# Weight slots 128 bytes instead of 64 bytes behind a multiple of 1024, in a one-core fp32 kernel of two model blocks

## What is computed

```python
# first block
h = rms_norm(x); proj = h @ w_in                       # 2048 x 6448
y = concat([rwkv7_mixer(proj_a), gdn_mixer(proj_b)])
x = x + y @ w_out                                      # 2048 x 2048
h = rms_norm(x)
x = x + (silu(h @ ffn_w_gate) * (h @ ffn_w_up)) @ ffn_w_down
x = rms_norm(x)
# second block
x = x + fox_mixer(rms_norm_2(x))                       # w_in 2048 x 6160, w_out 2048 x 2048
x = x + conv_ffn(rms_norm_2(x))                        # w_up 2048 x 11264, w_down 5632 x 2048
```

## Time and profile before

| | |
|---|---|
| median of three runs | 2491.35 us (2488.3 to 2492.03) |
| the profiled execution, its own time | 2490.99 us |
| its span, first to last instruction | 2489.3 us |
| mean granted TensorE clock | 0.995 of full |
| TensorE busy (matmul) | 2437.2 us |
| TensorE busy (weight loads, beside it) | 2409.3 us |
| VectorE, ScalarE, GpSimd busy | 1477.2, 1123.4, 114.8 us |
| moved by DMA | 431.72 MB, mean 173 GB/s |

### The profile page before, as it was taken

The page is one execution under the profiler, slowest core; times in us unless marked ns, Lnnn a source line. Parts: engine busy times, 40 slices in busy tenths (PEclk is TensorE's granted clock), DMA queues, the critical chain, the costliest instruction groups (busy, mean ns, idle before and its releaser), DMA issues.

```text
span 2489.3 us, 57370 instructions
## 1 busy us (share of the span) xinstructions
PE 2437.2 (98%) x24650; PEld 2409.3 (97%) x24650; DVE 1477.2 (59%) x1686; ACT 1123.4 (45%) x1064; POOL 114.8 (5%) x93
## 2 busy tenths in 40 slices
PE   8999989989999999999999999999999999999999
PEld 8999978889999999999999999989999999999998
DVE  5557588664654545554444567674576666765444
ACT  5333524444544444443344544363555555544332
POOL 3000050000200000000020100000200000000000
PEclk9999989999999999999999999999999999999999
DMA  7555300126555555556565565625555555555554
GB/s 233 187 193 195 119 2 4 37 86 188 197 191 192 196 186 197 190 191 196 188 198 191 188 239 200 221 83 188 187 199 189 191 197 186 197 190 190 197 190 150
DMA packets 171387, 431.72 MB, mean 173 GB/s; under 512 B 17614, under 2 KB 23387, under 8 KB 170107
## 3 DMA queue, kind: packets, MB, share of 16 engines
q1 hardware_dynamic: 170027, 422.30, 50.3%
q10 hardware_dynamic: 1232, 7.52, 0.8%
HBM read 427.59 MB, written 2.17 MB: 173 GB/s over the span
## 4 chain that ended last, share of the span: by engine, by line
PE 92%; DVE 6%; ACT 1%; POOL 1%; issue 0%; DMA 0%; DVEq 0%; SPq 0%; ACTq 0%; POOLq 0%
PE ps L1970 29%; PE ps L1971 29%; PE ps L1972 28%; PE ps L2124 1%; POOL SQ L528 1%; DVE TM L1366 0%; DVE LO L1370 0%; DVE TT L1367 0%; DVE CV L1400 0%; ACT HIW L606 0%; DVE LOW L1083 0%; DVE GT L1382 0%; PE ps L2162 0%; DVE TMP L1313 0%; PE ps L2068 0%
## 5 line engine op out<-in xcount | busy, mean ns | idle before, releaser
L1083 DVE TENSOR_TENSOR LOW<-RAW,HIW 128x2048 fp32r<-128x2048 f32 (+1 forms) x396 | 910.3, 2299 | 915.4 <-ACT HIW L606 915.4
L1970 PE MATMUL ps<-H_ROWS,HIW 128*128 128x256 f32 x4928 | 1366.7, 277 | 4.5 <-DVE H_ROWS L1122 1.3
L1971 PE MATMUL ps<-H_ROWS,HIW 128*128 128x256 f32 x4928 | 1365.6, 277 | 0.0
L1972 PE MATMUL ps<-H_ROWS,LOW 128*128 128x256 f32 x4928 | 1364.5, 277 | 0.0
L606 ACT ACTIVATE HIW<-RAW 128x2048 fp32r<-128x2048 f32 (+1 forms) x396 | 759.4, 1918 | 1180.1 <-PE ps L1972 1170.4
L1970 PEld LDWEIGHTS ps<-H_ROWS,HIW 128*128 128x128 f32 x4928 | 927.1, 188 | 6.2 <-issue 4.6
L1972 PEld LDWEIGHTS ps<-H_ROWS,LOW 128*128 128x128 f32 x4928 | 927.8, 188 | 0.0
L1971 PEld LDWEIGHTS ps<-H_ROWS,HIW 128*128 128x128 f32 x4928 | 926.5, 188 | 0.1
L1970 PE MATMUL ps<-HID,HIW 128*128 (+1 forms) x1408 | 388.7, 276 | 0.0
L1971 PE MATMUL ps<-HID,HIW 128*128 (+1 forms) x1408 | 388.6, 276 | 0.0
L1972 PE MATMUL ps<-HID,LOW 128*128 (+1 forms) x1408 | 388.6, 276 | 0.0
(11 more groups left out here) (367 smaller groups left out, 1514.1 us busy)
## 6 DMA issues: line engine op xcount, KB each, us to landing
RAW<-in_ffn_w_up SPq DMA_DIRECT2D x264, 512.0 KB, 4.3
RAW<-in_ffn_w_down SPq DMA_DIRECT2D x176, 512.0 KB, 4.8
RAW<-in_fox_w_in SPq DMA_DIRECT2D x98, 512.0 KB, 4.4
RAW<-in_w_in SPq DMA_DIRECT2D x96, 512.0 KB, 4.1
RAW<-in_ffn_w_gate SPq DMA_DIRECT2D x88, 512.0 KB, 3.6
RAW<-in_w_out SPq DMA_DIRECT2D x32, 512.0 KB, 5.0
RAW<-in_fox_w_out SPq DMA_DIRECT2D x32, 512.0 KB, 4.6
INV<-rows_out ACTq DMA_DIRECT2D x4, 1024.0 KB, 7.3
```

Of the source, the lines that this page charges most:

```text
L1083: V.tensor_tensor(LOW[:, u_const % 4, 0:n], RAW[:, u_const % 4, 0:n], HIW[:, u_const % 2, 0:n].bitcast(F32), ALU.subtract).then_inc(lo_mad ...
L1970: mm(o_, hi_w, h_hi, start=start, stop=False)
L1971: mm(o_, hi_w, h_lo, start=False, stop=False)
L1972: i = mm(o_, lo_w, h_hi, start=False, stop=stop)
```

## The change

Two offsets change from 64 to 128 bytes. The raw and low slots and all tensors with addresses relative to `w0` move up by 64 bytes, and so do the high slots. X, H_ROWS, HID and everything behind the 256 spare bytes stay where they are. The instructions, their order, their waits and the DMAs' sizes are the same.

```diff
-        w0 = o + 64
+        w0 = o + 128
         RAW = at("RAW", [P, RAW_SLOTS, UNIT], w0)
         LOW = at("LOW", [P, RAW_SLOTS, UNIT], w0, F32R); o += 32768
-        HIW = at("HIW", [P, HI_SLOTS, UNIT], o + 64, F32R); o += 16384
+        HIW = at("HIW", [P, HI_SLOTS, UNIT], o + 128, F32R); o += 16384
         o += 256
         h0 = o
```

## The result

The changed kernel takes **2577.61 us** (median of four runs, 2576.64 to 2580.07) against 2491.37 us for the kernel before (median of its four runs): **slower by 3.5%**, ratio 1.0347 with a 95% interval of 1.0334 to 1.0359. The forecast of 2491 us and the range that ended at 2568 us both missed it. The profiled execution took 2576.64 us, with a span of 2574.9 us, 85.6 us longer than before.

The account below looks back on a forecast made before the run. TensorE was taken to bound the kernel: 19,008 matmuls at 113.3 ns from start to start, plus small chained work. TensorE 0, splits 0, DMA 0 and the rest 0 +- 2.7 us gave 2491 us, range 2481 to 2568.

Parts of the forecast that it names:

- the price of 0 ns for TensorE's changed operand distance: Weight loop's 19,008 matmuls: start-to-start distance stays 113.3 ns, since nearest rows show no dependence at multiples of 64.
- VectorE's and ScalarE's pairs: Same operation at bases 64 bytes apart: 1225 against 1219 ns, and 1063 against 1063 ns; taken as no effect.
- under other offsets: Weights at 64 and 576, moving operands at 256 and 768 modulo 1024: one pace, 113.3 ns.
- the last tile: Tile k = 15, moving operand 240 bytes further on: its 24 matmuls take 119.2 ns each, 5.9 ns extra.
- 16 sums of squares: Matmuls with other weights, start off 64, at 116.9 ns each; cited for the slow pattern staying.
- Rival 1: Every weight matmul: slow pattern stays, 17,100 x 4.5 ns = 77 us, so 2568 us, or 2510 for HID only; chance 0.36.
- the paces seen: TensorE's bounds: up to 117.8 ns on all matmuls, down to 113.3 in slower places, at the far end 110.6 ns.
- The argument against: Against the slow pattern: once fast, the stream never falls back, and 64 to 128 keeps the line position inside 64.
- Rival 2: Weight loop: fast from the first matmul and last tile loses its extra, together 9.7 us, so 2481 us; chance 0.17.
- Rival 3: Weight loop: 113.3 ns is held up by a conflict; pace 110.6 ns, 51 us less, 2440 us; chance 0.04.
- Rival 4: If only the distance between raw, low and high slots mattered, nothing changes; inside the forecast, no chance of its own.
- The terms set to nothing: Splits 0, DMA 0, and the rest, recurrences and attention included, 0 +- 2.7 us.

Follow-up runs that it names:

- b1: The kernel before with LAST = 0 instead of 60, so the last tile is not set off; four runs took 2493.51 to 2541.8 us, ratio 1.0152.
- a2: The kernel before with weights moved from 64 to 0 and H_ROWS, HID and all behind from 256 to 192, distance kept at 192; 2494.81 us, ratio 1.001.
- a1: The kernel before with H_ROWS, HID and all behind 64 bytes earlier, weights left at 64, so distance 128; 2577.37 us, ratio 1.0345.
- b3: The kernel before with weights at 0 instead of 64 and H_ROWS left at 256, so distance 256; 2601.81 us.
- a3: The kernel before with the high slots alone moved from 64 to 128, raw and low slots left at 64; 2602.01 us, ratio 1.0445.

## Why the prediction was wrong

**The step that failed** is the price of 0 ns for TensorE's changed operand distance. The prediction had named the quantity (-192 to -128 modulo 512) and said that nothing showed its effect directly. It then took the nearest rows to be VectorE's and ScalarE's pairs and the pace "under other offsets". Those offsets (64 or 576 against 256 or 768) had one and the same distance modulo 256 in every case. Unchanged pace under them said nothing of another distance. The measured price is 5.33 ns on some 17,000 matmuls.

**The nearest row was the last tile**, the only matmuls of the weight loop with another distance, and it cost 5.9 ns. (The 16 sums of squares were a second sign: other weights, 116.9 ns.) By its own rule of going by the nearest row, the prediction should have given the bulk a price of several ns. It set the row aside, since 240 is no multiple of 64 and 64 bytes are. The runs show that a multiple of 64 protects from nothing: distances 0, 64 and 128 cost 6.7, 4.5 and 5.3 ns more than 192.

**Rival 1** named the side; it had been given 0.36. Its mechanism was right in that every matmul of the loop pays, in a pattern set by how the operands stand to each other. It was wrong in the pattern: it was not the slow pattern of the kernel before (117.8 ns) that held on; distance 128 has another one (118.7 ns). Hence 77 us forecast against 86 measured, and a range whose top, 2568 us, was the old slow pace and no bound at all. That top rested on "the paces seen" being the limits, though the last tile's 119.2 ns had been seen too. On 17,100 matmuls it gives 101 us, 2592 us, and would have held the result. The argument against, that the stream once fast never falls back in the trace of the kernel before, misread that trace. In its first group the starts of these two rows lie 57 matmuls apart:

```profile
21.21 0.28 PE L1970 MATMUL ps<-H_ROWS,HIW 128*128 128x256 f32 x1
...
27.67 0.28 PE L1970 MATMUL ps<-H_ROWS,HIW 128*128 128x256 f32 x1
```

That is 113.3 ns, and window 36:46 is slow again, 118.2 ns. The intervals go from 113 to 118 ns at 32.7 us, and none beside the change is above 124 ns; what turned it there is not known. b1 falls back as well, at its break at 61 us.

**Rival 2** foresaw that the last tile might lose its extra, and it did (119.2 to 114.7 ns), worth 4.0 us; it did not weigh that the bulk might trade places with it. **Rival 3**: none of the eight distances came below 113.3 ns. The Trainium skill, page "TensorE: Matmul & The Clock Gate", section "Back-to-back issue gap", gives N/2.4 + 2.5 ns, 109.2 ns for 256 columns, as the gap of a single matmul, without the weight loads beside it; no stretch of the weight loop in these runs reached it. **Rival 4** falls by the result itself: raw, low and high slots moved together and kept their distances, and the time rose by 3.5%. What may move together without a price is the slots and the moving operands (a2).

**The terms set to nothing** were nothing: the splits 2298 and 1913 ns, the recurrences and the attention 246.4 and 36.8 us against 246.5 and 36.8, the landings hidden. The Trainium skill, page "SBUF — State Buffer", section "Who interferes with whom", gives the moving operand and the weights two independent read ports. The prediction met this with doubt. The trace disagrees with it if independent is to mean that the addresses of one read do not matter to the pace beside the other: a1 and a2 show that they do, by 5.3 ns a matmul, and b3 by 6.7. Which circuit makes them do so, banks that both reads meet or another shared part, was not tried and stays open. That ScalarE and VectorE do not take part is shown between 900 and 1100 us: outside all splits the intervals average 118.7 ns in the changed kernel, beside a ScalarE or a VectorE split 118.6; in the kernel before they are 113.3 ns in all three cases. A slip without weight: the prediction's 2157 us and 332 us are worked out with 113.5 ns; with its own 113.3 ns they are 2154 and 336.

## What to carry to other kernels

Where back-to-back matmuls with fresh weights bound a kernel, the distance between the start of the weights and the start of the moving operand, modulo 256 bytes, is worth a scan: here 2% to 4.5% hang on it, with no change in instructions. Move the weights and the moving operands of the loop together when the memory map is changed, and do not mix distances without timing it (a3). Time a candidate in several runs and look at several stretches, since one distance can have two paces. In reading a profile, count matmuls in windows and not their mean duration, and where one tile alone runs at another pace, ask first what its addresses have that the others' do not.

## What was not expected of the hardware

- Distances 0 to 224 in steps of 32 bytes give 120.0, 116.7, 117.8, 120.0, 118.7, 117.3, 113.3 and 118.3 ns in the feed-forward, with neither a slope nor a rule in them that these runs show.
- At one distance two paces can each hold over two thousand matmuls and more, 113.3 and 117.8 ns, at a clock of 1.00 in both (b1_last0), and a break of 226 to 960 ns can turn the fast one into the slow one. That kernel's four runs, with the same instructions, spread over 48 us.
- High slots at distance 128 and low slots at 192 in one stream are slower (120.0 ns) than either distance alone (118.7 and 113.3 ns).
